# Sample attention of a hybrid decoder step: turned probabilities written over their scores, chunks taken in pairs, one sigmoid moved

## What is computed

```python
hid = per[:, :-1, 0] + per[:, 1:, 1] + bias[:, None, :]          # compress: windows of 32 rows, stride 16
out = jnp.einsum('bncgh,chd->bncgd', jax.nn.silu(hid), w2)       # compressed keys and values
o_cmp, idx = nsa_compressed(qq, tq, kc_b, vc_b, c_end, n_slc)    # attention on them, and the best 16 blocks of 64
p = masked_softmax(s, ...)                                       # attention on the chosen blocks ...
o = gg[:, 0] * o_cmp + gg[:, 1] * o_sel + gg[:, 2] * o_win       # ... and on the last 512 rows
```

## Time and profile before

| | us |
|---|---|
| median of 3 runs | 2159.87 |
| lowest and highest run | 2159.64, 2161.67 |
| the profiled execution | 2165.82 |
| its span | 2163.8 |
| PE busy in the span | 1993.5 (92%) |
| DVE, ACT, POOL busy | 838.9 (39%), 704.9 (33%), 128.3 (6%) |
| mean rate of the DMA queues | 145 GB/s |

### The profile page before, as it was taken

How to read it: one execution, slowest core, us unless ns; L and a number is a source line. 1 busy time by engine, 2 the same in 40 slices (tenths; PEclk the granted TensorE clock), 3 DMA queues, 4 the chain that set the end, 5 groups by cost and what they waited for, 6 DMA issues and landing times. The chain is left out here.

```text
span 2163.8 us, 37673 instructions
## 1 busy us (share of the span) xinstructions
PE 1993.5 (92%) x14849; PEld 1702.7 (79%) x14849; DVE 838.9 (39%) x1688; ACT 704.9 (33%) x1392; POOL 128.3 (6%) x244
## 2 busy tenths in 40 slices
PE   7999999999999798878999976999987599999998
PEld 7999999999999565557667653665554599989998
DVE  6233235523333244335444433445554322243232
ACT  6333223333333222212545533333343312132222
POOL 0000000000000101100000010221111011100000
PEclk9999999999999788868999988999997799999999
DMA  5552233333333414433344355888854822223320
GB/s 191 171 183 81 76 98 104 106 101 104 102 110 87 167 44 148 164 135 118 130 157 155 125 194 207 296 310 312 311 216 157 307 78 79 86 85 110 110 66 23
DMA packets 154355, 314.17 MB, mean 145 GB/s; under 512 B 18878, under 2 KB 68415, under 8 KB 151235
## 3 DMA queue, kind: packets, MB, share of 16 engines
q1 hardware_dynamic: 141208, 273.73, 37.9%
q0 software_dynamic: 11520, 37.76, 4.9%
q10 hardware_dynamic: 1450, 0.27, 0.1%
HBM read 279.70 MB, written 40.26 MB: 148 GB/s over the span
## 5 line engine op out<-in xcount | busy, mean ns | idle before, releaser
L257 PE MATMUL mm<-x_hi,w_hi 128*128 128x288 f32 x1696 | 368.9, 299 | 13.8 <-DVE w_lo L388 13.8
L257 PE MATMUL mm<-x_lo,w_hi 128*128 128x288 f32 x1696 | 364.3, 297 | 0.0
L257 PE MATMUL mm<-x_hi,w_lo 128*128 128x288 f32 x1696 | 364.2, 297 | 0.0
L257 PEld LDWEIGHTS mm<-x_hi,w_hi 128*128 128x128 f32 x1696 | 274.8, 190 | 15.4 <-issue 12.5
L388 DVE TENSOR_TENSOR w_lo<-w_raw,w_hi 128x1024 fp32r<-128x1024 f32 x106 | 129.8, 1225 | 385.2 <-ACT w_hi L287 385.2
L257 PEld LDWEIGHTS mm<-x_hi,w_lo 128*128 128x128 f32 x1696 | 274.2, 189 | 0.0
L257 PEld LDWEIGHTS mm<-x_lo,w_hi 128*128 128x128 f32 x1696 | 274.2, 189 | 0.0
L2039 PE MATMUL o_mm<-o_feat_hi,o_w_hi 128*128 128x288 f32 x1024 | 225.8, 303 | 25.2 <-DVE o_feat_lo L2114 17.7
L287 ACT ACTIVATE w_hi<-w_raw 128x1024 fp32r<-128x1024 f32 x106 | 112.1, 1058 | 343.2 <-PE mm L257 343.2
L2039 PE MATMUL o_mm<-o_feat_lo,o_w_hi 128*128 128x288 f32 x1024 | 221.7, 299 | 0.0
L2039 PE MATMUL o_mm<-o_feat_hi,o_w_lo 128*128 128x288 f32 x1024 | 221.6, 299 | 0.0
(11 more groups left out here) (416 smaller groups left out, 2422.4 us busy)
## 6 DMA issues: line engine op xcount, KB each, us to landing
wide<-pages SPq DMA_DIRECT2D x256, 256.0 KB, 4.5
w_raw<-w_in SPq DMA_DIRECT2D x106, 512.0 KB, 4.0
s_kv<-pages SPq DMA_DIRECT2D x128, 256.0 KB, 8.7
s_kv<-pages POOLq DMA_DIRECT2D x128, 256.0 KB, 6.9
o_w_raw<-w_out SPq DMA_DIRECT2D x16, 1024.0 KB, 8.1
o_w_raw<-ple_gate SPq DMA_DIRECT2D x16, 1024.0 KB, 6.9
m_state<-state SPq DMA_DIRECT2D x4, 2056.0 KB, 12.7
state_sample<-m_state SPq DMA_DIRECT2D x4, 2056.0 KB, 6.7
```

The lines of the kernel that those rows point to most:

```text
L257: last = nc.tensor.matmul(mm[:, s % 3, y, 0:HALF], w[:, m % RING, kk, :], f[:, k, y * HALF:(y + 1) * HALF], start=k == 0 and i == 0, stop= ...
```

## The change

The tile `probT` is taken away. DVE copies the turned chunk j back over chunk j of the scores tile, and PE reads it there (`turned_prob`); the turned new part goes over the first 128 columns of chunk 0, and its copy waits for the values of chunk 0. The copies no longer wait for earlier values. PE takes the chunks in pairs: turned 0, turned 1, then the last hidden step of the half unit (which stood ahead of turned 0), turned 2, turned 3, values 0, values 1, turned 4, turned 5, values 2, values 3, and so on to turned 8, values 6, values 7, values 8. ACT makes the next stream's sigmoid ahead of its wait for the maximum where the hidden sums are ready by then, which is so in streams 0 to 5; in stream 6 it stays between the exponentials.

```diff
--- before.py
+++ after.py
@@ -1493,7 +1493,6 @@
         hidg = sb("s_hidg", [P, KV, NC + 1])
         kcn, kcms = sb("s_kcn", [P, 2, KV * AD]), sb("s_kcms", [P, 2 * KV])
         kcT, vc = sb("s_kcT", [P, 2, 256]), sb("s_vc", [P, 2, KV * AD])
-        probT = sb("s_probT", [P, 2, 4, P])
         pgp, imp, top = sb("s_pgp", [32, 264]), sb("s_imp", [32, 72]), sb("s_top", [32, 2, 8])
         bias = sb("s_bias", [P, NBLK])
         mx, rs, col = sb("s_mx", [P, 16]), sb("s_rs", [P, 16]), sb("s_col", [P, 8])
@@ -1505,6 +1504,7 @@
         pwT = SC[:, 2048:2048 + 5 * P].rearrange("p (n r) -> p n r", r=P)
         csq = SC[:, 3072:3584]
         turn_t, spreadg = SC[0:TSA, 0:TS], SC[0:TSA, TS:TS + 3 * P].rearrange("p (y c) -> p y c", y=3)
+        turned_prob = lambda j, i: SC[:, j * CH + i * P:j * CH + (i + 1) * P] if j < NQ else SC[0:TSA, 0:P]
         chunk = lambda j: SC[:, j * CH:(j + 1) * CH] if j < NQ else SC[:, PAST:PAST + TSA]
         newmask = lambda b: B.newmask[:, b * TSA:(b + 1) * TSA]
         gate = sig[:, 0:NH]
@@ -1674,10 +1674,10 @@
                         rows, own = slice(32 * g, 32 * g + 32), half(g % 2)
                         if q < NQ:
                             v0 = 256 + g * AD
-                            last = mm(pO[rows, 0, own], probT[:, q % 2, i, rows], kvp[:, 4 * q + i, v0:v0 + AD],
+                            last = mm(pO[rows, 0, own], turned_prob(q, i)[:, rows], kvp[:, 4 * q + i, v0:v0 + AD],
                                       start=q == 0 and i == 0, stop=False)
                         else:
-                            last = mm(pO[rows, 0, own], probT[0:TSA, q % 2, 0, rows], B.vsel_new[:, g * AD:(g + 1) * AD],
+                            last = mm(pO[rows, 0, own], turned_prob(NQ, 0)[:, rows], B.vsel_new[:, g * AD:(g + 1) * AD],
                                       start=False, stop=True)
                 last.then_inc(pv_done, 1)
 
@@ -1716,12 +1716,16 @@
                     scores(b, j)
                     if j in (2, 4, 6):
                         hidden(b, 3, range(1 + j // 2, 2 + j // 2))
-                hidden(b, 3, range(5, 8))
-                for j in range(PARTS + 1):
-                    if j < PARTS:
-                        turned(b, j)
-                    if j >= 1:
-                        values(b, j - 1)
+                hidden(b, 3, range(5, 7))
+                for j in range(0, PARTS + 2, 2):
+                    for t in (j, j + 1):
+                        if t < PARTS:
+                            turned(b, t)
+                    if j == 0:
+                        hidden(b, 3, range(7, 8))
+                    for q in (j - 2, j - 1):
+                        if 0 <= q < PARTS:
+                            values(b, q)
             gather(NB - 1)
 
         @block.scalar
@@ -1780,11 +1784,15 @@
                 s_.activation(pwT[:, 0:4, :], pT[:, 0, :].rearrange("p (n r) -> p n r", r=P), ACT.Copy)
                 s_.activation(pwT[0:TSA, 4, :], pT[0:TSA, 1, 256:256 + P], ACT.Copy).then_inc(wt_ready, 1)
                 split(b, 2)
+                ready = 4 * (c + 1) <= UNITS_EARLY + 2 * b
+                for part in range(3):
+                    if ready:
+                        sigmoid(c, part)
                 act.wait_ge(mx_ready, b + 1)
                 for j in range(PARTS):
                     if j == 2:
                         split(b, 3)
-                    if j in (4, 5, 6):
+                    if j in (4, 5, 6) and not ready:
                         sigmoid(c, j - 4)
                     s_.activation(chunk(j), chunk(j), ACT.Exp, bias=mx[:, 11:12], accum_out=rs[:, j:j + 1]).then_inc(p_ready, 1)
             act.wait_ge(B.win_kept, 16 * NB)
@@ -1900,12 +1908,11 @@
                 v.tensor_reduce(mx[:, 11:12], mx[:, 0:PARTS], AX, ALU.max, negate=True).then_inc(mx_ready, 1)
                 for j in range(PARTS):
                     dve.wait_ge(t_done, PARTS * b + j + 1)
-                    if j >= 2:
-                        dve.wait_ge(pv_done, PARTS * b + j - 1)
                     if j < NQ:
-                        last = v.tensor_copy(probT[:, j % 2], pT[:, j % 2, :].rearrange("p (n r) -> p n r", r=P))
+                        last = v.tensor_copy(chunk(j), pT[:, j % 2, :])
                     else:
-                        last = v.tensor_copy(probT[0:TSA, j % 2, 0, :], pT[0:TSA, j % 2, 0:P])
+                        dve.wait_ge(pv_done, PARTS * b + 1)
+                        last = v.tensor_copy(turned_prob(NQ, 0), pT[0:TSA, j % 2, 0:P])
                     last.then_inc(t_copied, 1)
                     if j in (0, 2):
                         added(b, j // 2)
```

## The result

| | before | after |
|---|---|---|
| median of 8 runs each, us | 2159.76 | 2173.67 |
| lowest and highest | 2155.02, 2162.31 | 2170.05, 2187.31 |
| profiled execution, us | 2165.82 | 2174.79 |
| its span | 2163.8 | 2172.7 |

The changed kernel is slower by 13.9 us, a ratio of 1.0073 with a 95% interval of 1.0051 to 1.0094. The forecast was 2179.7 in a range of 2167 to 2195: the side and the range hold, the size is 6.0 us too large, and the first rival (no clock drops, 2173.7) names the measured time.

The account below looks back on a forecast made before the run. The prediction took two equally long chains to bound each stream: PE's own work, and hidden matmul, SP, pages, scores of chunk 4. Page delays 12.4 + stream 6 1.4 + clock drops 6 = 19.8 us, giving 2179.7 us, range 2167 to 2195.

Parts of the forecast that it names:

- the first rival: Samples' attention: slower by the same delays but without clock drops, 13.8 us, 2173.7 us; chance 0.26.
- Two chains that close each stream: Each 46 us stream: PE's own work, and hidden matmul, SP, pages, scores of chunk 4, are equally long.
- SP 7.4 us after the first exponential, POOL 14.5: Load queues: SP's "wide" loads start at 7.4 us instead of 5.0, POOL's s_kv loads at 14.5 instead of 12.1.
- Waits of L1650, 12.4 us more: Scores of chunk 4, waiting for later pages: 12.4 us added over six streams, between 11 and 14.
- The loop gains nothing: Loop of turned chunks and values: early sigmoid is paid back by late split and block order; ends 0.1 us later.
- Stream 6, +1.4: Stream 6 keeps its sigmoid between the exponentials; turned 2 moves 1.4 us and takes both along, adding 1.4 us.
- Clock drops at the stalls, 3 x 2 = 6 us: PE stalls before the scores of chunk 4: three of six drop the clock, 2 us each, 6 us.
- The rival "absorbed": Page loads: bandwidth sets landing, so later issue is absorbed; only stream 6's 1.4 us remains, 2161.3 us; chance 0.06.
- The rival "faster": Loop end: the product at L1806 no longer holds copy 7, 0.85 us saved in six streams, 2154.8 us; chance 0.05.

Follow-up runs that it names:

- e2: The kernel before with only the last hidden step moved behind turned 1; 2167.89 us, ratio 1.0031.
- e3: The kernel before with only the next stream's sigmoid put ahead of the wait for the maximum in streams 0 to 5; 2157.12 us, ratio 0.998.
- e13: e3 with DVE's product of sigmoid and hidden values moved right behind the maximum in streams 0 to 5; 2155.2 us, ratio 0.9978.
- e11: The changed kernel with SP loading only 64 of 512 columns per page of each stream's second hidden unit; 2171.53 us, ratio 1.0049.
- e7: The kernel before with SP and POOL reading page numbers before their waits; 2160.46 us, ratio 0.9996.
- e8: The changed kernel with hidden step and sigmoid back at their old places, leaving pairs and write-back; 2173.89 us, ratio 1.0056.
- e10: e6 with turned chunks and values alternating one by one instead of in pairs; 2155.35 us, ratio 0.9969.
- e6: e1 with SP and POOL reading page numbers before their waits; 2173.12 us, ratio 1.0053.
- e1: The changed kernel with only the last hidden step put back ahead of turned 0; 2160.99 us, ratio 0.9995.
- e9: e3 with SP and POOL reading page numbers before their waits; 2156.45 us, ratio 0.9974.
- e5: The changed kernel with SP and POOL reading page numbers before their waits; 2176.91 us, ratio 1.0066.

## Why the prediction was right, and where its sizes were off

- **Two chains that close each stream**: right. e2, e3 and e13 show it from either side: a shorter loop comes back as page waits (2.6 and 8.0 us), a longer one hides them (0.6).
- **SP 7.4 us after the first exponential, POOL 14.5**: measured 7.2 and, in streams 1 to 4, 13.9 to 14.2. POOL's term was 0.6 too large, since the loop was faster than I had it.
- **Waits of L1650, 12.4 us more**: the weight loads wait 11.3 us more, PE itself 8.6. I took the weight load's wait as PE's; the matmuls in flight cover about a fourth of it. The rest of the periods grew by 0.1, 1.9, 3.2, 1.3, 1.6 and 1.6 us, 9.7 in all, where I had 2.1, 1.3, 2.1, 2.4, 2.1 and 2.4: the first is missing because the loop of stream 0 was longer, the second late group in the period of stream 2 was not in my sum.
- **The loop gains nothing**: wrong by 0.45 us in streams 1 to 4 (13.5 for 13.95). Turned 2 came 4.35 us after the first exponential (forecast 4.57), and blocks of the same kind take 0.51 us, not 0.59; I had carried the pace of the alternating order over to the pairs. The 1.8 us bought nothing in these streams: PE came sooner to pages that were later.
- **Stream 6, +1.4**: loop +1.55. The first sigmoid comes 6.1 us behind the first exponential instead of 5.0, about what I had for it; the other 0.4 us cannot be put down to one cause, since in both kernels a part of this loop runs at the lower clock.
- **Clock drops at the stalls, 3 x 2 = 6 us**: this is the term that failed. At after's page stalls the clock was 1.00, as above; one in e11 did drop. The drops of after stand in the gap ahead of turned 2, a pause of 1.7 us of PE that my own arithmetic contained (hidden step done at 1526.10, turned 2 at 1527.82) and that I did not price. With an idle on issue of 1.6 us in stream 0 they made the loops of streams 0 and 5 longer by 3.7 us. Against the 13.5 us of streams 1 to 4 that is 1.3 us for the drop in stream 5, and 1.7 for the one in stream 0 without the idle, near my 2. That three drops were forecast and three came is luck. Why the same gap of 1.70 us loses the clock in three loops and keeps it in four, and why the stalls at L1650 kept it here, stays open.
- **The rival "absorbed"**: refuted by the 15.5 us of waits. The Trainium skill, "DMA: Bandwidth & Descriptors", section "Issuing engines are not separate DMA queues", calls the sequencer's time usually small relative to the transfer. In these traces it is not: a shift of 2.2 us in SP's queue arrives as waits of about 2 us, and with the numbers read ahead of the wait the pages land some 4 us earlier (e7 against before). Nor did less traffic ahead of those pages help (e11).
- **The rival "faster"**: its mechanism (the product at L1806 holds the last values) is real, and e13 shows it from the other side; its price is bounded by the pages, as the prediction said.
- **Not foreseen**: that the pair order itself costs. e8 alone (12.5 us over its before) and e10 against e6 (17.8) show it, but the costs do not add: with sigmoid and step at their best, pairs and write-back cost 3.9 us (e3 to e1). In the changed kernel itself only 2.9 us of idles on issue are seen; its loss is for the most part the moved step, as e1 shows.

What stays open: how much of the 17.8 us between the orders is the stops alone, and how much the lower clock behind them. That traffic makes the packets late is shown by the delays above (0.5 and 2.8 us), and by the idles that rise from 2.1 to 16.9 us when nothing but the start of the loads moves (e1, e6), and from 0 to 4.6 (e3, e9). It is not a matter of when SP starts alone: e8 has 8.7 us with SP's loads at the old place (POOL's start 2.2 us later).

## What to carry to other kernels

Before an instruction is moved behind others, look at who waits for it on other engines and queues: here one hidden matmul step of 0.7 us carried a copy, an exponential and 24 loads, and its move was worth 6.5 us in one kernel and 14.3 in the other. A loop that closes two chains of equal length gains from an edit only up to the other chain; measure both, and shorten both together. When an engine idles in the middle of a run of small instructions and waits for nothing, count instructions from one such stop to the next before looking for a data dependence.

## What the runs showed of the hardware that I had not expected

PE's program comes in packets of 16.4 KB, 256 instructions, through the same DMA engines as the data. A packet starts a median of 0.5 us after PE passes a 256th instruction when the DMA engines are idle and 2.8 us when they are full, and PE can go on 2.2 us after that at the earliest in the stops seen. Its stops lie a multiple of 256 instructions apart, up to 3.87 us each (in e5, `L1682`), and 17 us in all over seven loops where 128 small instructions stand in 1.03 us and the pages land at the same time; in the same kernel with alternating blocks they are 5.5 us. Two blocks of the same kind back to back took 1.03 us, two of different kinds 1.17.
